# Eight or eleven high products, then as many low ones: the order of the matmuls within a weight chunk of a float32 decoder trunk

## What is computed

```
def swiglu(h, w_gate, w_up, w_down):
    return (jax.nn.silu(h @ w_gate) * (h @ w_up)) @ w_down

for l in range(DEPTH):                      # DEPTH = 2, one layer of each kind
    if l == N_A:
        k_nope, k_pe, v = shared_mla_kv(rms_norm(x, kv_in_norm), w_kv_a,
                                        kv_latent_norm, w_kv_b, cos, sin)
    if l < N_A:
        x = x + multiscale_pool_mixer(rms_norm(x, pool_norm[l]), pool_w[l], pool_scale[l])
    else:
        x = x + mla_layer_mixer(rms_norm(x, attn_norm[b]), ..., w_o[b], k_nope, k_pe, v, cos, sin)
    x = x + swiglu(rms_norm(x, ffn_norm[l]), w_gate[l], w_up[l], w_down[l])
return rms_norm(x, final_norm)
```

## Time and profile before

| | |
|---|---|
| median of 3 runs | 1788.62 us (1788.32 to 1788.66) |
| profiled execution, whole | 1790.32 us |
| its span, first to last instruction | 1788.5 us |
| TensorE busy, share of the span | 1766.2 us, 99% |
| VectorE busy | 1140.5 us, 64% |
| ScalarE busy | 914.7 us, 51% |
| mean granted TensorE clock | 0.996 of full speed |

### The profile page before, as it was taken

How to read it: one execution, slowest core, us unless ns; L and a number is a source line. 1 busy time by engine, 2 the same in 40 slices (tenths; PEclk the granted TensorE clock), 3 DMA queues, 4 the chain that set the end, 5 groups by cost and what they waited for, 6 DMA issues and landing times.

```text
span 1788.5 us, 29487 instructions
## 1 busy us (share of the span) xinstructions
PE 1766.2 (99%) x10424; PEld 1565.0 (88%) x10424; DVE 1140.5 (64%) x1438; ACT 914.7 (51%) x1177; POOL 133.2 (7%) x162
## 2 busy tenths in 40 slices
PE   9999999999999999999999999999999999999996
PEld 5888888888888888888999888888888888888886
DVE  5766666556666666678987776666655566666554
ACT  5666664334444444455775456666533344444442
POOL 2100000000000001123112420000000000000112
PEclk9999999999999999999999999999999999999998
DMA  7555557545555566544444555555665455556541
GB/s 264 176 191 188 188 189 241 187 161 174 188 188 188 190 226 198 172 147 136 150 145 153 190 187 189 189 192 188 222 204 165 165 188 192 191 189 227 192 159 47
DMA packets 84141, 327.16 MB, mean 183 GB/s; under 512 B 9472, under 2 KB 9728, under 8 KB 84096
## 3 DMA queue, kind: packets, MB, share of 16 engines
q1 hardware_dynamic: 84096, 326.57, 54.2%
HBM read 324.43 MB, written 2.10 MB: 183 GB/s over the span
## 4 chain that ended last, share of the span: by engine, by line
PE 96%; DVE 2%; ACT 1%; DMA 0%; issue 0%; POOL 0%; SPq 0%; DVEq 0%; ACTq 0%
PE ps L386 58%; PE ps L387 31%; PE ps L459 1%; PE ps L394 1%; PE ps L396 1%; PE ps L395 1%; DMA raw<-pool_w 0%; PE ps L581 0%; PE ps L580 0%; PE ps L582 0%; DVE xg L1106 0%; PE ps L631 0%; DVE w_lo L1096 0%; DVE y L1473 0%; PE ps L650 0%
## 5 line engine op out<-in xcount | busy, mean ns | idle before, releaser
L386 PE MATMUL ps<-xg,w_hi 128*128 128x512 f32 x2880 | 1001.5, 391 | 2.2 <-DVE xg L1106 1.7
L1096 DVE TENSOR_TENSOR w_lo<-raw,w_hi 128x1024 fp32r<-128x1024 f32 (+2 forms) x561 | 734.4, 1311 | 417.4 <-ACT w_hi L745 416.6
L745 ACT ACTIVATE w_hi<-raw 128x1024 fp32r<-128x1024 f32 (+2 forms) x562 | 630.8, 1124 | 496.5 <-PE ps L387 495.0
L387 PE MATMUL ps<-xg,w_lo 128*128 128x256 f32 x2880 | 812.8, 282 | 0.0
L386 PEld LDWEIGHTS ps<-xg,w_hi 128*128 128x128 f32 x2880 | 541.5, 188 | 116.6 <-DVE xg L1106 2.7
L387 PEld LDWEIGHTS ps<-xg,w_lo 128*128 128x128 f32 x2880 | 545.1, 189 | 0.1
L386 PE MATMUL ps<-act,w_hi 128*128 128x512 f32 x1408 | 488.3, 390 | 0.0
L387 PE MATMUL ps<-act,w_lo 128*128 128x256 f32 x1408 | 397.1, 282 | 0.0
L386 PEld LDWEIGHTS ps<-act,w_hi 128*128 128x128 f32 x1408 | 264.4, 188 | 55.4
L387 PEld LDWEIGHTS ps<-act,w_lo 128*128 128x128 f32 x1408 | 266.1, 189 | 0.0
L1501 POOL TENSOR_TENSOR square<-x 128x256 f32 (+1 forms) x47 | 42.4, 902 | 1459.7 <-DVE x L1201 1459.7
(11 more groups left out here) (176 smaller groups left out, 1175.8 us busy)
## 6 DMA issues: line engine op xcount, KB each, us to landing
raw<-w_gate SPq DMA_DIRECT2D x176, 512.0 KB, 3.2
raw<-w_up SPq DMA_DIRECT2D x176, 512.0 KB, 3.2
raw<-w_down SPq DMA_DIRECT2D x128, 704.0 KB, 4.2
raw<-w_o SPq DMA_DIRECT2D x32, 512.0 KB, 3.2
raw<-pool_w SPq DMA_DIRECT2D x8, 512.0 KB, 11.3
raw<-w_q_a SPq DMA_DIRECT2D x8, 512.0 KB, 3.2
raw<-w_kv_a SPq DMA_DIRECT2D x8, 512.0 KB, 3.2
raw<-w_q_nope SPq DMA_DIRECT2D x8, 512.0 KB, 3.2
```

The costliest lines, as they stand in the source:

```text
L386: pe.matmul(ps[:, bank, :], w_hi[:, s, j * P:(j + 1) * P], moving, start=start, stop=False)
L387: return pe.matmul(ps[:, bank, 0:SEQ], w_lo[:, s, j * P:(j + 1) * P], moving[:, 0:SEQ], start=False, stop=stop)
L745: nc.scalar.activation(dst, src, ACT.Copy).then_inc(hi_ready, 1)
L1096: nc.vector.tensor_tensor(lo, src, hi.bitcast(F32), ALU.subtract).then_inc(lo_ready, 1)
```

## The change

Within a chunk TensorE now issues all high products and then all low ones. The wait for `lo_ready` ahead of the chunk becomes a wait for `hi_ready`, and a wait for `lo_ready` stands ahead of the low products. The waits for single pieces of the activations stand ahead of the high products, as before. `product3` and `long_tile`'s argument `product` go; a new `chunk_product` does this for `long_tile`, `first_tiles` and `wo_part`. The tile `kpe` uses `product_two` for its high products: two matmuls of 256 columns for each piece. `product_one` stays for the heads' own projections. No other engine's program changes.

```diff
-            def product3(n, j, bank, moving, start, stop):
-
-                s = n % SPLIT_SLOTS
-                pe.matmul(ps[:, bank, :], w_hi[:, s, j * P:(j + 1) * P], moving, start=start, stop=False)
-                return pe.matmul(ps[:, bank, 0:SEQ], w_lo[:, s, j * P:(j + 1) * P], moving[:, 0:SEQ],
-                                 start=False, stop=stop)
+            def product_hi(n, j, bank, moving, start):
+
+                w = w_hi[:, n % SPLIT_SLOTS, j * P:(j + 1) * P]
+                return pe.matmul(ps[:, bank, :], w, moving, start=start, stop=False)
+
+            def product_two(n, j, bank, moving, start):
+
+                w = w_hi[:, n % SPLIT_SLOTS, j * P:(j + 1) * P]
+                pe.matmul(ps[:, bank, 0:SEQ], w, moving[:, 0:SEQ], start=start, stop=False)
+                return pe.matmul(ps[:, bank, 0:SEQ], w, moving[:, SEQ:], start=False, stop=False)
+
+            def product_lo(n, j, bank, moving, stop):
+
+                w = w_lo[:, n % SPLIT_SLOTS, j * P:(j + 1) * P]
+                return pe.matmul(ps[:, bank, 0:SEQ], w, moving[:, 0:SEQ], start=False, stop=stop)
+
+            def chunk_product(n, bank, operand, k0, kts, first, last, i=None, each=None, own=product_hi):
+
+                pe.wait_ge(hi_ready, plus(made(n), i, BODY))
+                for j in range(kts):
+                    if each is not None:
+                        each(k0 + j)
+                    own(n, j, bank, operand[:, k0 + j, :], first and j == 0)
+                pe.wait_ge(lo_ready, plus(made(n), i, BODY))
+                for j in range(kts):
+                    mm = product_lo(n, j, bank, operand[:, k0 + j, :], last and j == kts - 1)
+                return mm
...
                 for c in range(2):
-                    pe.wait_ge(lo_ready, plus(made(n + c), i, BODY))
                     if c == 0:
                         bank_free(t, i, per)
-                    for j in range(kts):
-                        kt = c * kts + j
-                        if each is not None:
-                            each(kt)
-                        mm = product(n + c, j, t % 4, operand[:, kt, :], kt == 0, kt == 2 * kts - 1)
+                    mm = chunk_product(n + c, t % 4, operand, c * kts, kts, c == 0, c == 1, i, each, own)
                     mm.then_inc(chunks_used, 1)
```

More of the change, by code:

```diff
@@ L422, in first_tiles @@
                         continue
-                    pe.wait_ge(lo_ready, made(n + c))
                     if half == 0:
@@ L428, in first_tiles @@
                             bank_free(t + m)
[L429 to L433 removed]
+                    mm = chunk_product(n + c, (t + m) % 4, xg, half * TILES, TILES, half == 0, half == 1, None,
+                                       (lambda kt: pe.wait_ge(xg_ready, xg_before + kt + 1)) if m == 0 else None)
                     mm.then_inc(chunks_used, 1)
@@ L555, in _ @@
             long_tile(CHUNK["kpe"], TILE["kpe"], xk, TILES, each=lambda kt: latent_stats() if kt == TILES else None,
-                      product=product_one)
+                      own=product_two)
             def key_part(g, i=None):
@@ L658, in wo_part @@
                 half = c // 4 % 2
-                pe.wait_ge(lo_ready, plus(made(n), i, BODY))
                 if half == 0:
                     bank_free(t, i, 4)
-                for j in range(TILES):
-                    kt = half * TILES + j
-                    if each is not None:
-                        each(kt)
-                    mm = product3(n, j, t % 4, heads[:, kt, :], kt == 0, kt == DT - 1)
+                mm = chunk_product(n, t % 4, heads, half * TILES, TILES, half == 0, half == 1, i, each)
                 mm.then_inc(chunks_used, 1)
```

7 lines of the change are left out of this document (1 added, 6 removed).

## The result

The changed kernel took **1810.15 us** (median of 4 runs, 1808.16 to 1810.7), the kernel before 1788.64 us beside it (4 runs, 1788.32 to 1788.73): a ratio of **1.0114**, 95% interval 1.0102 to 1.0127. It is slower by 21.5 us, where 2.3 us were forecast, and outside of the range. The profiled execution took 1810.7 us.

What follows compares the result with a forecast made beforehand. The prediction took TensorE's distance from matmul to matmul to bound the kernel. Regrouping 0, waits 0 and awaited activation pieces 0.82 + 0.82 + 0.68 gave +2.3 us, 1790.9 us, called no change; range 1783.5 to 1798 us.

Steps and rivals of the forecast that it cites:

- What bounds the kernel: Weights are always ahead of TensorE; the distance between matmuls counts, 346.6 ns a pair, 4608 pairs, 1597 of 1788.5 us.
- Part 1: Regrouping high and low products inside each chunk: each step depends on its own width alone, so cost 0.
- The 229.7 ns: Inferred step of a 512-column high product: 346.6 ns a pair less 116.9 for a 256-column step in a run.
- The line through 60, 116.9 and 229.7 ns: Steps of 128, 256 and 512 columns lie on one line within a nanosecond, taken as no price for changing width.
- The bound above, 1.7 ns: Upper bound on a step's change either way, from 256-column records: 282 ns in pairs, 280.3 in latent products.
- The sign of being wrong: A high-to-high step off 230 ns by more than a third of a nanosecond, either way, would refute the forecast.
- Part 2: New waits for `hi_ready` and `lo_ready` in each chunk are met long before: cost 0.
- Part 3: Low products postponed where activation pieces are awaited: 0.82 us first gate and up, 0.82 first `kva`, 0.68 `wo_part(4)`, `down` 0.
- A change of width costs something: Rival: 4080 pairs each save 1.7 ns by regrouping, 6.9 us, giving 1784.0 us; chance 0.12.
- A run at 216 ns: Rival: high products in a run step at 216 ns, saving 57 us, about 1734 us; chance 0.05.
- Low products short of their loads: Rival: weight loads no longer fit under 256-column matmuls in a row, 1.7 ns x 4080, 1797.8 us; chance 0.14.
- One more stretch at half clock: Rival: TensorE idles more at the first tiles, another half-clock stretch costs 1.6 us or somewhat over, 1792.6 us; chance 0.09.

Runs made afterwards that it cites:

- the two timed kernels: The changed kernel, 1810.15 us, and one that regroups only chunks waiting for activation pieces one by one, 1792.83 us (ratio 1.0018 to the kernel before).
- the held chunk: The kernel before, plus repeated products of one kept `w_q_a` chunk into an unused bank, other engines idle: 346.7 ns a pair in turn, 350.0 in runs.

## Why the prediction was wrong

**What bounds the kernel: right.** All of the loss is the distance between matmuls, and a nanosecond a pair is 4.6 us, as said.

**Part 1 was the step that failed**: "I take each step to depend on its own width alone, and the regrouping costs 0". It costs 3.8 ns a pair by the count of the stretch, 17.5 us in all, and 18.6 us by the two timed kernels. Three things were wrong in it.
- The 229.7 ns were a difference between a step in a run (116.9) and a pair in which no step is that of a run. The steps in turn are 228.3 and 118.3, as the starts in the trace of before would have shown: with 116.9 for the low product, the high one seemed 1.4 ns dearer than it was. The 118.3 already differs from the run's 116.9 by 1.4 ns, the hint that the neighbour counts; I took the pair as a whole and never read its two steps apart. These steps alone do not foretell 233.3, though.
- The line through 60, 116.9 and 229.7 ns was a coincidence. Alone on the core, with other operands, 256 columns take 120.0 and 512 take 226.7 ns; with the kernel's own operands, 116.7 and 233.3. The first pair differs by 106.7, which is 256 columns at the 26.7 ns for 64 read above; the second by 116.7. What is on top of the columns thus is 13.3 for both widths there, and 10 and 20 here. That is the part that order and placement move.
- The bound above, 1.7 ns, was taken from the durations of 256-column records. A high product's step grew by 5 ns. The rows had no 512-column run of this format, and a bound from another width was no bound. The sign of being wrong that was named, a high-to-high step off 230 ns by more than a third of a nanosecond, came: it was 233.3.

**Part 2, the waits: right.** With both waits and the old order the ratio is 1.000, and 2310 matmuls stand in the stretch.

**Part 3, the pieces of the activation: right in mechanism, and near in size.** 2.9 us were measured for it alone against 2.3. The terms were 0.84 for `xk` against 0.82 and 0.62 for `wo_part(4)` against 0.68. The down phase cost nothing, as forecast. What answers to the earlier trace rows in the changed kernel:

```profile
298.83 2.73 PE L386 MATMUL ps<-act,w_hi 128*128 128x512 f32 x11
301.40 1.45 PE L397 MATMUL ps<-act,w_lo 128*128 128x256 f32 x11
```

```profile
302.54 0.42 DVE L1197 TENSOR_TENSOR act<-product,act 128x256 fp32r<-128x256 f32 x1 [0.48 <-ACT act L839]
```

The second chunk begins at 298.83 + 11 x 0.35 = 302.68, its eleventh high product ten steps of 233 ns later, at 305.0; the last piece of `act` is there at 302.96.

At the first tiles it was more than the 0.82: the half-clock stretch grew from 3.4 to 6.8 us, for another 1.0. That stretch appears in some executions and not in others (the profile of the kernel in turn with both waits has none there, but its first `xg` product starts 1.6 us later). That part of the 2.9 stands for how often it comes is likely, and not shown.

**The rivals.** *A change of width costs something*, forecast as faster: in this placement the opposite is so, a change of width saves 3.8 ns a pair; with the activations 32 bytes further on it costs 8.9, and the changed kernel then is at 1783.9 us, next to that rival's 1784.0, by another mechanism; the nearness is luck. *A run at 216 ns*: nothing came near; the lowest mean step from one 512-column product to the next is 226.7. That plain float32 streams its columns twice for each record was not tested. Each call there leaves two records (L459 has 64 for 32 calls), so a plain float32 matmul of 512 columns takes some 860 ns. The Trainium skill's rule of 215.8 ns for 512 columns ("TensorE: Matmul & The Clock Gate", section "Back-to-back issue gap"), which it gives for isolated matmuls, holds in no series here, each of whose matmuls loads new weights of the split format, or the same again (226.7, too). *Low products short of their loads*: the sign was right, the place was not. The low products became faster (117 against 118.3) and the high ones slower, and the price was 3.8 ns, not 1.7. *One more stretch at half clock*: it happened as well, as a longer stretch, for 1.0 us where 1.6 were named.

**The range** ended at 1798 because the bound of part 1 did. A difference of order had a price per pair that no row of the trace gave, times 4080. Such a step needed a range of 5 ns a pair on both sides, some 20 us, and a chance of "no change" much under 0.6.

## What to carry to other kernels

In this kernel, where TensorE is busy all the time, the order of products of different widths and the distance in SBUF between the weights and the moving operand together set the distance between matmuls, from 344.5 to 353.4 ns a pair, 2.6%. Neither can be judged by itself: try an order with the buffers in two or three placements (a pad of 32 bytes was enough here) before keeping or dropping it. And read each kind of step from the starts in the trace by its two neighbours; a step whose neighbour never occurs there is unknown, and no line through other widths replaces it.

## What the runs showed of the hardware

- With weights and moving operand in SBUF, a 32-byte pad between them changed the kernel before by +1.1% and the changed one by -1.4% (from 1.0114 to 0.9969 of the unpadded kernel before). It is their distance that counts, as far as was tried. That the reads of the two operands get in each other's way is a likely reason, but it is only argued: no run shows the reads. The rule for the distance is open (ten offsets gave no simple period).
- One width by itself takes 233.3 ns for 512 columns in the kernel and in the held chunk and 228.9 with the pad, and 116.7 and 117.8 for 256. With pieces of `act` as weights it takes 226.7 and 120.0.
- At the granted clock of 0.50 a 512-column product took 426 ns and a pair 640, against 233 and 350 at full clock.
- The padded kernel before spread over 1800.6 to 1819.4 us with one program on one chip, while all others kept within 4 us. Its profiled execution held 353.4 ns throughout the stretch. Why its executions differ is open; another steady rhythm, met in some of them, would do it, but no second profile was taken.
- Groups of two cost nothing with 8 pieces a chunk (346.7) and 3.6 ns with 11 (350.3 against 346.7), where a chunk ends with a single pair.
